# Second block written out flat: layer norms applied behind six projection units, one gate piece, two conv-projection pieces

## The reference, cut to what matters

```python
h = layer_norm(concat(meta, rms_norm(x, final_norm)), ln_in_g, ln_in_b)
for l in range(2):
    proj = h @ w_in[l]                       # 2048 x 5120: c_val c_glu c_gate q k v a_gate r_x r_gate
    c = c_val * sigmoid(c_glu)
    c = silu(layer_norm(causal_conv31(c)))   # 512 channels, 31 taps
    y_conv = (c @ conv_pw_w + b) * silu(c_gate)
    y_attn = window_attention(rope(q), rope(k), v, sinks) * silu(a_gate)   # 16 heads of 64, 4 kv heads
    r = causal_conv4(r_x)
    y_lru = rg_lru(r, wa, wx, lambda) * silu(r_gate)
    h = layer_norm(alpha * h + concat(y_conv, y_attn, y_lru) @ w_out[l], g, b)
return h[:, 16:]
```

## Time and profile before

| | us |
|---|---|
| median of 3 runs (2968.75 to 2972.76) | 2970.13 |
| the profiled execution's own time | 2972.88 |
| its span, first to last instruction | 2971.1 |
| TensorE busy | 2811.0 (95%) |
| VectorE busy | 1886.4 (63%) |
| ScalarE busy | 1358.3 (46%) |
| GpSimd busy | 286.7 (10%) |

### The profile page before, as it was taken

One profiled execution on the slowest core, in us unless ns is written; L12 is line 12 of the kernel. 1 busy time (PEld: TensorE's weight loads), 2 busy tenths in 40 slices (PEclk: granted clock), 3 DMA queues, 4 the chain that ended last, 5 costly groups with the idle time before them and its releaser, 6 DMA issues.

```text
span 2971.1 us, 48151 instructions
## 1 busy us (share of the span) xinstructions
PE 2811.0 (95%) x17485; PEld 2510.7 (85%) x17485; DVE 1886.4 (63%) x2404; ACT 1358.3 (46%) x1903; POOL 286.7 (10%) x234
## 2 busy tenths in 40 slices
PE   7999999999999999999999999986999896999895
PEld 6888888888888888888888887876988896998895
DVE  6655656565655556666666666556797755788665
ACT  4544444444544444444444444433344634344633
POOL 0000000000000011010101010002033101014101
PEclk8999999999999899999999999998999998999997
DMA  6555555555555265555555554543533452543352
GB/s 186 178 179 179 178 182 179 178 179 179 170 174 188 87 200 181 175 182 178 179 180 178 182 179 157 183 137 114 168 122 107 126 183 76 178 137 107 114 175 71
DMA packets 477396, 474.37 MB, mean 160 GB/s; under 512 B 17736, under 2 KB 473056, under 8 KB 477280
## 3 DMA queue, kind: packets, MB, share of 16 engines
q1 hardware_dynamic: 474112, 472.08, 51.6%
q10 hardware_dynamic: 3184, 0.93, 0.1%
HBM read 470.82 MB, written 2.13 MB: 159 GB/s over the span
## 4 chain that ended last, share of the span: by engine, by line
PE 79%; issue 11%; DVE 5%; ACT 2%; POOL 2%; ACTq 0%; DMA 0%; DVEq 0%; POOLq 0%; SPq 0%
PE proj L1015 31%; PE proj L1017 16%; PE proj L1030 8%; PE proj L1196 4%; PE proj L1032 4%; PE proj L1197 4%; PE proj L1198 4%; DVE w_both L1400 1%; PE ps_t L1188 1%; PE ps_s L1092 1%; PE ps_s L1075 1%; POOL x_res L584 1%; ACT w_both L647 1%; PE ps_t L1082 1%; POOL x_res L586 1%
## 5 line engine op out<-in xcount | busy, mean ns | idle before, releaser
L1400 DVE TENSOR_TENSOR w_both<-w_raw,w_both 128x1024 fp32r<-128x1024 f32 x868 | 1107.2, 1279 | 923.9 <-ACT w_both L647 921.1
L647 ACT ACTIVATE w_both<-w_raw 128x1024 fp32r<-128x1024 f32 x868 | 917.8, 1059 | 1273.4 <-PE proj L1017 716.5
L1015 PE MATMUL proj<-operand,w_both 128*128 128x512 f32 x4096 | 1466.8, 402 | 16.3 <-DVE operand L1474 10.1
L1017 PE MATMUL proj<-operand,w_both 128*128 128x256 f32 x4096 | 1151.8, 281 | 0.0
L1015 PEld LDWEIGHTS proj<-operand,w_both 128*128 128x128 f32 x4096 | 774.2, 189 | 204.8 <-issue 14.2
L1017 PEld LDWEIGHTS proj<-operand,w_both 128*128 128x128 f32 x4096 | 778.1, 190 | 0.8
L1196 PE MATMUL proj<-operand,w_both 128*128 128x272 f32 x1840 | 543.7, 295 | 52.6 <-DVE operand L1698 26.5
L1197 PE MATMUL proj<-operand,w_both 128*128 128x272 f32 x1840 | 539.4, 293 | 0.0
L1198 PE MATMUL proj<-operand,w_both 128*128 128x272 f32 x1840 | 537.8, 292 | 0.0
L1196 PEld LDWEIGHTS proj<-operand,w_both 128*128 128x128 f32 x1840 | 355.1, 193 | 62.4 <-DVE operand L1698 27.4
L1030 PE MATMUL proj<-w_both,operand 128*128 128x512 f32 x1024 | 364.7, 400 | 4.8 <-DVE w_both L1400 4.8
(11 more groups left out here) (281 smaller groups left out, 1926.6 us busy)
## 6 DMA issues: line engine op xcount, KB each, us to landing
w_raw<-in_a_w_in_dram SPq DMA_DIRECT2D x256, 512.0 KB, 3.7
w_raw<-in_w_in_dram SPq DMA_DIRECT2D x164, 512.0 KB, 3.6
w_raw<-in_b_w_in_dram SPq DMA_DIRECT2D x128, 512.0 KB, 3.8
w_raw<-in_kv_w_dram SPq DMA_DIRECT2D x128, 512.0 KB, 3.8
w_raw<-in_a_w_out_dram SPq DMA_DIRECT2D x64, 512.0 KB, 4.1
w_raw<-in_b_w_out_dram SPq DMA_DIRECT2D x64, 512.0 KB, 4.5
w_raw<-in_w_out_dram SPq DMA_DIRECT2D x64, 512.0 KB, 3.4
scratch<-in_a_rel_bias_dram SPq DMA_DIRECT2D x16, 256.0 KB, 3.7
```

The source lines that it names most:

```text
L647: act.activation(w_hi[:, s], w_raw[:, s], ACT.Copy).then_inc(hi_ready, 1)
L1015: pe.matmul(proj[:, 2 * bank + t, :], w_hi[:, s, kk, cols], rhs[:, k, :], start=first and k == 0, stop=False)
L1017: m = pe.matmul(proj[:, 2 * bank + t, 0:S], w_lo[:, s, kk, cols], rhs[:, k, 0:S], start=False, stop=last and end)
L1400: dve.tensor_tensor(w_lo[:, s], w_raw[:, s], w_hi[:, s].bitcast(F32), ALU.subtract).then_inc(pieces_split, 1)
```

## The change

The second block and its two layers are written out flat. Weight pieces are counted one by one over the layer (115 per layer instead of 30 units of four): `hi(n)`, `lo(n)` and `next_split` take the next n.

1. **Norms behind raw units.** The first six units (val, glu, k, v: 24 pieces) multiply raw x, which is the un-normed x times the gain, 274 columns wide: two columns more hold -gain and shift, whose products (`raw_sides`) are taken out with the unit. The norm runs beside them on VectorE and ScalarE (the squares are first added up to four tiles, so 4 matmuls instead of 16; all 16 tiles' gain and shift on ScalarE). VectorE repairs the raw outputs with `fix` (times 1/std, plus mean/std times the side column), ScalarE adds the other side column. The rest of the units use the normed x as before. The raw parts are made in the last unit of the first block, and of layer 0, as `raw_his`, `raw_los`.
2. **Loads moved**: both layers' vectors and taps and the constants (13 small DMAs) are issued before the first weight piece of the second block.
3. **Attention**: scores are negated and the two heads interleaved, so the meta keys of both heads are turned together (9 transposes for 12) and multiplied together (one product for two); the copy of the turned meta probabilities goes from VectorE to ScalarE, and so do the divisions and the sinks.
4. **Taps**: recurrent taps go from GpSimd to ScalarE (first) and VectorE (three); the first conv tap from VectorE to ScalarE.
5. **Recurrent gates** are one piece within the seventh pair's unit; sigmoids are taken over all tiles at once. **Conv projection** is two pieces behind one and a half output units; unit order is r_x, r_gate, a_gate, c_gate. The end of the layer has a new order on all engines.
6. The last norm, behind layer 1, stays as it was.

```diff
-U_VAL, U_K, U_V, U_Q, U_RX, U_CGATE, U_AGATE, U_LRU, U_RGATE, U_PW, U_OUT, UNITS_2 = 0, 4, 5, 6, 10, 12, 14, 18, 19, 21, 22, 30
+N_LRU, N_PW, LAYER_PIECES = 67, 86, 115
+RAW_T = T + 2
...
 # TensorE
+                for chunk in range(PIECES):
+                    pe.wait_ge(raw_split, OUT_N * l + 2 * chunk + 2)
+                    pieces(0, raw, (chunk,), RAW_T)
+                    if chunk == 1:
+                        mean_sums()
+                pieces(1, raw, (0, 1, 2, 3), RAW_T)
+                pieces(2, raw, (0, 1), RAW_T)
+                square_sums()
+                pieces(2, raw, (2, 3), RAW_T)
+                for unit in range(3, RAW_UNITS):
+                    pieces(unit, raw, (0, 1, 2, 3), RAW_T)
...
+                pieces(U_Q + 2, norm, (0,))
+                turn_values()
+                pieces(U_Q + 2, norm, (1,))
+                double_meta_values()
...
+                for group in range(3):
+                    pe.wait_ge(y_split, 7 * l + 2 + group)
+                    pieces(O_OUT, y, (group,))
+                pieces(O_OUT + 1, y, (0, 1))
+                pe.wait_ge(y_split, 7 * l + 5)
...
+                pieces(O_OUT + 1, y, (2,))
+                pe.wait_ge(y_split, 7 * l + 7)
+                pieces(O_OUT, y, (3,))
+                pieces(O_OUT + 1, y, (3,))
...
 # VectorE, raw part of a layer (fix of glu, k, val, v)
+                def fix(dst, units, done):
+                    tiles = dst.shape[1]
+                    step(dve.tensor_tensor(dst, dst, over(ln_rstd, tiles), ALU.mult))
+                    for t in range(tiles):
+                        m = dve.scalar_tensor_tensor(dst[:, t, :], ln_mu_rstd, raw_sides[:, units + t // 2, t % 2, 0:1], dst[:, t, :],
+                                                     ALU.mult, ALU.add)
+                    m.then_inc(done, 1)
...
 # VectorE, q units
+                lo(2)
+                add_taps(TAPS_DURING[0])
+                lo(1)
+                copy_values()
...
 # VectorE, end of a layer
+                lo(1)
+                y_lo_of(3, att[:, 4:8, :], slice(4, 8))
+                silu_of(3, r_gates, r_gates)
+                dve.tensor_tensor(lru_t, lru_t, r_gates, ALU.mult).then_inc(y_ready, 1)
+                lo(1)
+                dve.wait_ge(c_root_ready, l + 1)
+                step(dve.reciprocal(c_rstd, c_rstd))
+                step(refine(c_rstd, c_mean, c_mu))
+                dve.tensor_tensor(conv, conv, over(c_rstd, CT), ALU.mult).then_inc(c_scaled, 1)
+                lo(1)
+                y_lo_of(4, lru_t, slice(8, 12))
+                lo(1)
+                silu_of(4, conv, conv)
...
 # ScalarE, pairs
+                def divide_by_sums(i):
+                    act.wait_ge(recip_2_ready, PAIRS_2 * l + i + 1)
+                    for h in range(2):
+                        act.activation(s2[:, 0:144, h], s2[:, 0:144, h], ACT.Copy, scale=sums_2[:, 0, h:h + 1])
+                        act.activation(s2[:, 146:418, h], s2[:, 146:418, h], ACT.Copy, scale=sums_2[:, 1, h:h + 1])
+                        m = act.activation(sm[0:META, 0:META, h], sm[0:META, 0:META, h], ACT.Copy, scale=sums_2[0:META, 2, h:h + 1])
+                    m.then_inc(p_2_ready, 1)
```

More of the change, by code:

```diff
@@ L4 @@
 from concourse import mybir
+import itertools
 import numpy as np
@@ L77, in shape_constants @@
     parts["tri"] = (q <= k).astype(np.float32)
+    head = np.arange(P) % 2
+    parts["twice"] = (q == np.arange(4 * META)[None, :] // 2).astype(np.float32)
+    parts["head_of"] = np.stack([(head == e).astype(np.float32) for e in range(2)], 1)
     chunked = np.where(k < (q // CHUNK + 1) * CHUNK, 0.0, NEG).astype(np.float32)
@@ new lines, in _ @@
+                for half in range(2):
+                    act.wait_ge(y_ready, 4 * l + 3 + half)
+                    hi_of(conv[:, 2 * half:2 * half + 2, :], slice(12 + 2 * half, 14 + 2 * half))
+                hi(2)
+                for j in range(OUT_N):
+                    if j == 1:
+                        hi(1)
+                    elif j >= 2 and (l + 1 < DEPTH or j < OUT_N - 1):
+                        hi(4)
+                    if l + 1 < DEPTH:
+                        act.wait_ge(proj_free, o0 + O_OUT + j + 3)
+                        raw_his(l + 1, (j,))
@@ new lines, in _, with conv_square_sums @@
+                pe.wait_ge(conv_tap, TAPS * (l + 1))
+                pe.wait_ge(neg_max_ready, PAIRS_2 * l + 8)
+                for t in range(CT):
+                    m = pe.matmul(ps_s[:, 0, 0:T], ones, conv[:, t, :], start=t == 0, stop=t == CT - 1)
+                m.then_inc(c_summed, 1)
+                pieces(U_CGATE, norm, (1,))
+                head_values(7)
+                pieces(U_CGATE, norm, (2, 3))
+                def conv_square_sums(half):
+                    pe.wait_ge(c_squared, 2 * l + half + 1)
+                    for t in range(2):
+                        m = pe.matmul(ps_s[:, 1, 0:T], ones, conv_sq[:, t, :], start=half + t == 0, stop=half + t == 2)
+                    m.then_inc(c_sq_summed, 1)
@@ new lines, in _ @@
+                pe.wait_ge(y_split, 7 * l + 7)
+                pieces(O_OUT, y, (3,))
+                pieces(O_OUT + 1, y, (3,))
+                for j in range(2, OUT_N):
+                    pieces(O_OUT + j, y, (0, 1, 2, 3))
+            n = DEPTH
+            pe.wait_ge(ln_summable, OUT_N * n + 1)
+            pe.matmul(ps_t[:, 0, 0:T], ones, ln_sums[:, 0, :], start=True, stop=False)
+            pe.matmul(ps_t[:, 0, 0:T], ones, ln_sums[:, 1, :], start=False, stop=True).then_inc(ln_summed, 1)
@@ new lines, in _ @@
+                lo(1)
+                y_lo_of(5, conv, slice(12, 16))
+                lo(1)
+                step(dve.memset(ln_sums, 0.0))
+                if l + 1 < DEPTH:
+                    raw_parts_los(l + 1)
+                silu_of(5, c_gates, c_gates)
+                lo(2)
+                for half in range(2):
+                    rows = slice(2 * half, 2 * half + 2)
+                    dve.wait_ge(pw_taken, 2 * l + half + 1)
+                    dve.tensor_tensor(conv[:, rows, :], conv[:, rows, :], c_gates[:, rows, :], ALU.mult).then_inc(y_ready, 1)
@@ L1924, in mixed @@
+                for half in range(2):
+                    y_lo_of(6 + half, conv[:, 2 * half:2 * half + 2, :], slice(12 + 2 * half, 14 + 2 * half))
+                lo(2)
+                def mixed(j):
                     output = o0 + O_OUT + j
-                    dve.wait_ge(pieces_used, PIECES * (unit + 2))
+                    bank = 2 * (output % 2)
+                    dve.wait_ge(pieces_used, p0 + last_out_piece(j) + 1 + PIECES)
                     dve.wait_ge(proj_free, output + 2)
-                    xs = x_res[:, bass.ds(2 * j, 2), :]
```

1422 lines of the change are left out of this document (825 added, 597 removed).

## The result

The changed kernel takes 2906.0 us (median of 4 runs, 2904.8 to 2909.6) against 2969.4 for the one before on the same chip: a ratio of 0.978, 95% interval 0.977 to 0.980. The prediction was 2878, its range 2846 to 2910. The time lies in the range, at its upper end. The terms do not bear it out as well as that: the layers lose 41 us more than the sum has, and 18 us come back in terms that the sum also had wrong. That the time lies inside the range is in part luck.

The account below looks back on a forecast made before the run. TensorE's order of work bounds the layers, the norm's chain the stretches between. First block 1990.3 + border 8 + 2 x 390.8 work + 2 x 24.6 waits + last norm 50.1 = 2879.2 span; forecast 2878 us, range 2846 to 2910.

Parts of the forecast that it names:

- border: Between the blocks: 8 us for a wait, the norm's sums, row transposes and a restart partly at half clock.
- last norm: Behind layer 1: last norm and output carried over from the old profile at 50.1 us.
- Rival E: Norm not hidden, as repairs and normed parts end as late as before: 2958, up to 2973 us; chance 0.03.
- rival D: Raw units' 274-wide products leave the column rate; at twice the time 144 us more, 3022 us; chance 0.04.
- The wait in the q units: In the q units TensorE waits about 2.4 us for turned values, copied behind VectorE's three taps and a split.
- The end of a layer: After a layer's last pair TensorE waits 16 us for low parts of y that VectorE makes late.
- Half clock: At the end of each layer, 2.5 us for TensorE at the lower clock after the longest wait there.
- First pairs: In the first pairs of heads, where VectorE's taps and the rest fill its time: 1.5 us of waits a layer.
- Seventh pair: In the seventh pair, waits for ScalarE's take of the fourth gate tile and for its sigmoids: together 2.2 us.
- Pieces: TensorE's 112 full pieces a layer at 3.0 us, 336.0, plus 0.5 for the raw units' two extra columns.
- Pair work: A pair of heads costs TensorE 3.8 us instead of 4.36, by fewer transposes and one meta product.
- rival B: VectorE's order costs more (q units, first pairs, layer's end): 40 us of waits a layer, 2908 us; chance 0.16.

Follow-up runs that it names:

- e6: Changed kernel with the recurrent branch's four taps back on GpSimd as eight 1088-wide operations: 2925.0 us.
- e1: Changed kernel with the normed input and y in rows of 272 numbers (1088 bytes) again, raw input still 274: 2906.7 us.
- e3: Changed kernel with three moves in ScalarE's and VectorE's order in the middle of a layer: value copies, taps and small steps, seventh pair: 2901.7 us.
- e7: Changed kernel with ScalarE's and VectorE's work reordered both in the middle and at the end of a layer: 2871.1 us.
- e2: Changed kernel with four high and four low parts of the normed x, which nothing reads, put back behind the last norm: 2913.5 us.
- e9: The changed kernel itself, unaltered, measured again beside later experiments: 2908.7 us.
- e11: e7 with e1's rows, and layer 0's sixteen small VectorE steps in four parts behind pairs 1, 3, 4 and 5: 2867.3 us.
- e10: Changed kernel with matmuls whose result nothing reads ahead of TensorE's four waits at the end of a layer: 2901.8 us.

## Why the prediction was right, and where it was not

Against the profile's 2902.7 the sum of 2879.2 is short by 23.5 us: first block's end -0.9, border -4.2, layer 0 +22.8, layer 1 +18.4, last norm -12.6.

**Right.** The norms are hidden: no wait for `in_split`, and only 1.6 and 0.6 us for the square sums. Rival E is out. The raw units stand 0.127 us a matmul; rival D is out. The wait in the q units is 2.43 us in both layers (2.4 predicted). The 8.6 us beside GpSimd's taps left with them, as e6 shows. The end of a layer loses 13.7 and 13.9 us in named waits for the low parts of y, in the places foreseen (16). Table loads are 8 in layer 1 (about 9 predicted) and take 1.28 us; ScalarE's next work starts 1.30 us behind the start of one (2258.38 and 2259.68). The flat code, for which the sum had nothing, shows no price in the pitch of the matmuls (e1).

**Wrong in size, in each layer** (layer 0, layer 1):
- Half clock. The sum had 2.5 us a layer. It was 12.7 and 11.2: 1.6 behind the q units' wait, 1.5 behind the first pair's in layer 0, 2.5 in the seventh pair, 7.1 at the end. This term of the sum, "2.5 for half clock after the longest", is the largest error, 9 to 10 us a layer. All four waits at the end of a layer, each of over 2 us, had it behind them, not the longest alone. Its size is that of one execution.
- First pairs: 5.36 and 2.16 us, 1.5 predicted. I had counted VectorE's taps, not that two taps, and in layer 0 the small steps, stand ahead of the first pair's maxima.
- Seventh pair: 4.7 us, 2.2 predicted. I had the takes late, but not `copy_head_outputs`, which queued behind exponentials, a split, divisions and sinks. e3 removed that wait.
- Pieces: 340.0 us, 336.5 predicted. I priced the two extra columns in the raw units alone; e1 shows that the longer row costs 0.001 us a matmul in all the others too, 2.2 of these 3.5 us.
- Pair work 4.0 us, 3.8 predicted. The one wide meta product takes as long as the two narrow ones did: 0.65 us to the next product, 0.61 before (2193.36 to 2193.97).

These give 21.9 and 16.8 us. The square sums add 1.6 and 0.6, other takes 0.6 and 1.1, and the end takes 2.3 and 2.1 away. That makes 21.8 and 16.4 of the 22.8 and 18.4 us; the last 1.0 and 2.0 have no name.

**Wrong the other way.** The border kept its clock and waited half as long: 3.8 us, not 8. (In e7's profile the clock fell there too.) And the last norm was carried over at 50.1 us, though the unrolled layers drop the splits behind it (e2: 8.2 us).

With 42 and 38 us lost beside TensorE's work in the layers, the number that came true there is rival B's, 40, not the forecast's 24.6. B's mechanism fits in part. The end of a layer lost 7.1 us to half clock, where B had 7.5, and the first pair of layer 0 lost 3.9 us more than forecast. But the wait in the q units was what the forecast had, and the seventh pair, which lost 2.5 us more and as much at half clock, is in no rival. The 41 us too few in the layers met 18 us too many outside them. Without these 18 the time would have been 2924 us, above the range; that they were there was luck. The chance of 0.16 for B was too low.

**Open.** Whether the clock falls behind a wait is not settled by the wait's length. Behind the first pair's wait in layer 1 it stayed at 1.00 in the changed kernel (2.16 us), and in e9, the same program, it fell (2.17 us). Busy us of TensorE, count, granted clock, DMA share, first the changed kernel, then e9:

```profile
2588.00:2596.00 8.00, 7.90 (x62) 1.00 0.63 197
2594.00:2602.00 8.00, 7.91 (x49) 0.79 0.64 196
```

At the border it fell in e7 behind a wait of 1.21 us, which it did not in the changed kernel:

```profile
1994.00:2002.00 8.00, 7.30 (x40) 0.79 0.43 132
```

So what half clock costs differs between executions of one program, and a single profile gives it to 4 us at best. Nor was it tried whether it is the length of the rows or where each row starts that costs the 0.001 us of e1.

## What to carry to other kernels

Where one engine's order is fixed and two others serve it, price a wait with the pieces behind it: here what was lost at half clock came to nearly half of the named waits (12.7 us on 28.4 in layer 0, in one profile). List, for every result that the bound engine waits for, what stands ahead of it in its own engine's queue and could as well stand behind it; such moves, with e1's rows, gave 1.4% (e11 against e9), two thirds of what the change itself gave. And when a loop is unrolled, look in its last pass for work that only the loop's form required.

## What the runs showed of the hardware

- A moving operand whose rows are 1096 bytes apart costs 0.0010 us a matmul of 272 columns against 1088 bytes (0.1262 and 0.1251 us), at the same granted clock of 1.00.
- A VectorE split took 1.2 us alone and 3.2 beside GpSimd's 1088-wide operations, four taps 1.7 and 5.7 (e6).
- Matmuls that compute nothing kept TensorE's clock at its upper level through a wait; behind 2.2 us of idle time after them it was at the lower one again (e10).
- The same wait of 2.2 us in the same program was followed by the lower level of the clock in one execution (0.79 over 8 us, e9) and not in another (1.00, the changed kernel).
